# A two-layer decoder trunk in split float32: the order of the rounded-weight and remainder products within a weight piece

## The reference

```python
for i in range(DEPTH):                      # DEPTH = 2
    h = _rmsnorm(x, attn_norm_g[i])
    # layer 0: stick-breaking attention, layer 1: sparse attention with a top-k of keys
    x = x + mix
    h = _rmsnorm(x, ffn_norm_g[i])
    x = x + _conv_ffn(h, ffn_w_up[i], ffn_conv_w[i], ffn_conv_b[i], ffn_w_down[i])
```

## Time and profile before

| | before |
|---|---|
| median of three runs | 2218.34 us (2217.62 to 2219.71) |
| span of the profiled execution, first to last instruction | 2216.0 us |
| what lies between that span and the median | 2.3 us |
| PE busy | 2209.4 us, 12470 matmuls |
| PEld busy | 1935.2 us, 12470 loads |
| DVE busy | 1484.4 us |
| ACT busy | 1177.3 us |
| bytes read from memory | 408.42 MB, 185 GB/s over the span |
| granted TensorE clock | 1.000 of full speed over the span |

### The profile page before, as it was taken

How to read it: one execution, slowest core, us unless ns; L and a number is a source line. 1 busy time by engine, 2 the same in 40 slices (tenths; PEclk the granted TensorE clock), 3 DMA queues, 4 the chain that set the end, 5 groups by cost and what they waited for, 6 DMA issues and landing times.

```text
span 2216.0 us, 34772 instructions
## 1 busy us (share of the span) xinstructions
PE 2209.4 (100%) x12470; PEld 1935.2 (87%) x12470; DVE 1484.4 (67%) x1753; ACT 1177.3 (53%) x1409; POOL 14.3 (1%) x21
## 2 busy tenths in 40 slices
PE   9999999999999999999999999999999999999999
PEld 8888898888888888888899888888888888888887
DVE  7666556677777777555578888667777777774443
ACT  7565555555555555444455466555555555553333
POOL 0000000000000000000010000000000000000000
PEclk9999999999999999999999999999999999999999
DMA  7555555555555555565566544555555656566664
GB/s 270 166 168 177 171 162 181 195 185 190 189 193 186 189 190 191 190 190 189 191 212 198 177 157 139 161 183 191 182 198 181 194 184 198 180 193 201 201 199 136
DMA packets 113829, 411.55 MB, mean 186 GB/s; under 512 B 12769, under 2 KB 13537, under 8 KB 113761
## 3 DMA queue, kind: packets, MB, share of 16 engines
q1 hardware_dynamic: 112320, 406.70, 56.5%
q10 hardware_dynamic: 1008, 2.30, 0.3%
q0 software_dynamic: 432, 1.57, 0.2%
HBM read 408.42 MB, written 2.10 MB: 185 GB/s over the span
## 4 chain that ended last, share of the span: by engine, by line
PE 99%; DMA 0%; SPq 0%; DVE 0%; ACT 0%; issue 0%; DVEq 0%
PE psum L1301 99%; DMA raw<-w_all 0%; PE psum L1621 0%; PE psum L1557 0%; DVE w_lo L747 0%; ACT w_hi L289 0%; SPq L237 0%; SPq L235 0%; DVE upad L822 0%; SPq L236 0%; SPq L234 0%; DVEq L83 0%
## 5 line engine op out<-in xcount | busy, mean ns | idle before, releaser
L747 DVE TENSOR_TENSOR w_lo<-raw,w_hi 128x1024 fp32r<-128x1024 f32 x769 | 935.6, 1224 | 678.6 <-ACT w_hi L289 672.8
L1301 PE MATMUL psum<-xg,w_hi 128*128 128x512 f32 (+1 forms) x3936 | 1358.3, 392 | 1.9 <-DVE w_lo L747 1.0
L289 ACT CAST w_hi<-raw 128x1024 fp32r<-128x1024 f32 x770 | 803.1, 1049 | 771.4 <-PE psum L1301 767.6
L1301 PE MATMUL psum<-xg,w_lo 128*128 128x256 f32 (+1 forms) x3920 | 1090.8, 278 | 0.0
L1301 PEld LDWEIGHTS psum<-xg,w_hi 128*128 128x128 f32 x3936 | 736.0, 187 | 156.7 <-issue 2.2
L1301 PEld LDWEIGHTS psum<-xg,w_lo 128*128 128x128 f32 x3920 | 742.6, 189 | 2.6 <-issue 2.2
L1301 PE MATMUL psum<-hid,w_hi 128*128 128x512 f32 x704 | 244.1, 391 | 0.0
L1301 PE MATMUL psum<-w_hi,hid 128*128 128x512 f32 x704 | 217.9, 390 | 0.0
L1301 PE MATMUL psum<-hid,w_lo 128*128 128x256 f32 x704 | 197.4, 280 | 0.0
L1301 PE MATMUL psum<-att,w_hi 128*128 128x512 f32 x512 | 178.8, 393 | 0.0
L1301 PEld LDWEIGHTS psum<-hid,w_hi 128*128 128x128 f32 x704 | 131.7, 187 | 28.6
(11 more groups left out here) (176 smaller groups left out, 1062.9 us busy)
## 6 DMA issues: line engine op xcount, KB each, us to landing
raw<-w_all SPq DMA_DIRECT2D x770, 512.0 KB, 3.8
xres<-x_in SPq DMA_DIRECT2D x3, 512.0 KB, 9.0
cst<-consts_in ACTq DMA_DIRECT2D x2, 768.0 KB, 6.6
raw<-w_all SPq DMA_DIRECT2D x2, 256.0 KB, 3.6
xres<-x_in SPq DMA_DIRECT2D x2, 256.0 KB, 3.8
out_t<-part POOLq DMA_DIRECT2D x1, 512.0 KB, 7.3
out_t<-conv POOLq DMA_DIRECT2D x1, 512.0 KB, 7.4
out_t<-gates POOLq DMA_DIRECT2D x1, 512.0 KB, 7.0
```

What stands on the lines that cost most here:

```text
L289: act.copy(w_hi[:, c % RING, :], raw[:, c % RING, :]).then_inc(hi_ready, 1)
L747: dve.tensor_tensor(w_lo[:, c % RING, :], raw[:, c % RING, :], f32(w_hi[:, c % RING, :]), ALU.subtract).then_inc(lo_ready, 1)
L1301: return pe.matmul(o, lhsT, rhs, start=start, stop=True, skip_group_check=True)
```

## The change

Within `proj` the two products of a tile no longer follow each other. One loop over the eight tiles issues all products with `w_hi`, a second loop over the same tiles all products with `w_lo`. The waits for `xg_tile`, for `lo_ready` in the first piece and for `upper_free` stand in the first loop. `last`, which raises `piece_used`, is the last short product as before. No other function is touched.

```diff
                 s = c % RING
-                for ct in range(cols // P):
-                    if ct == 2 and upper_free is not None:
+                tiles = [(ct, kk) for ct in range(cols // P) for kk in range(kts)]
+                for ct, kk in tiles:
+                    if ct == 2 and kk == 0 and upper_free is not None:
                         pe.wait_ge(*upper_free)
-                    for kk in range(kts):
-                        w = slice(kk * cols + ct * P, kk * cols + (ct + 1) * P)
-                        k = k0_ + kk
-                        if by_tile and ct == 0 and kk == 2:
-                            pe.wait_ge(lo_ready, c + 1)
-                        if by_tile and ct == 0:
-                            pe.wait_ge(xg_tile, kk + 1)
-                        mm(psum[:, bank0 + ct, :], w_hi[:, s, w], act_in[:, k, :], first and kk == 0)
-                        last = mm(psum[:, bank0 + ct, 0:T], w_lo[:, s, w], act_in[:, k, 0:T])
+                    if by_tile and ct == 0 and kk == 2:
+                        pe.wait_ge(lo_ready, c + 1)
+                    if by_tile and ct == 0:
+                        pe.wait_ge(xg_tile, kk + 1)
+                    w = slice(kk * cols + ct * P, kk * cols + (ct + 1) * P)
+                    mm(psum[:, bank0 + ct, :], w_hi[:, s, w], act_in[:, k0_ + kk, :], first and kk == 0)
+                for ct, kk in tiles:
+                    w = slice(kk * cols + ct * P, kk * cols + (ct + 1) * P)
+                    last = mm(psum[:, bank0 + ct, 0:T], w_lo[:, s, w], act_in[:, k0_ + kk, 0:T])
                 last.then_inc(piece_used, 1)
```

## The result

The changed kernel takes 2227.96 us (median of five runs, 2227.63 to 2228.24) against 2217.62 us for the kernel before beside it: ratio 1.0046, 95% interval 1.0035 to 1.0057. It is slower by 10.3 us, where no difference that can be measured was forecast, and 3 us above the stated range.

The account below looks back on a forecast made before the run. TensorE's start-to-start gaps were taken to bound the kernel. Regrouping was worth 0 in steady stretches, edges and waits 0: 2216.0 us span less 2.3 is 2213.7, plus 2.3 to the median gives 2216.0 us, range 2208 to 2225.

Parts of the forecast that it names:

- pure gaps: Start-to-start gaps on TensorE among products of one length: 226.7 ns for 512 columns, 120.0 ns for 256; 2773 ns a piece.
- slow threes: About 115 stretches where three alternating pairs take 1.06 us, 20 ns lost each; forecast to go, gaining 2.3 us.
- The wait moved in layer 1's output projection: First piece, ahead of the fifth long product, now reached about 1385.89 us; cost forecast 0, at most 0.4 us.
- the edges of the runs: Where short and long runs meet in a piece: forecast between -7 and +10 ns a piece, taken as 0.
- Rival 2: Slower: the local pattern of 353.3 ns a pair takes hold at every edge from short to long; 2248.5 us, chance 0.10.
- the full pattern: 353.3 ns a pair instead of 346.67 taking hold everywhere: 6.67 ns x 4880 = 32.5 us.
- The reason given for 0: At a piece's edges, what a product gains at one edge it has lost at the other in the alternation also.
- The waits at the head: First piece: up to three short products (0.36 us) fall behind waits for the normed input's rows; cost forecast 0.
- the cover of 1.17 us: Time PE waits anyway behind the first piece for the next piece's remainders, set against 0.36 us of moved products.
- The rule on load shares: Busy share of weight loads measures TensorE's nearness to its limit; short runs would then have gaps of 188 ns.

## Why the prediction was wrong

**What held.** PE's gaps bind, waits played no part, and the pure gaps are what they were read as: 227 ns and 120 ns come back late in each run. The slow threes went, as forecast. The wait moved in layer 1's output projection cost nothing; no such wait is in the trace.

**The step that failed** is the edges of the runs: "Added, the two edges of a piece lie between -7 and +10 ns by the nearest rows [...] I take 0, because what a product gains at one edge it has lost at the other in the alternation also." Measured, they add to +20 ns. Each edge was read for one gap, and that gap was read rightly: the long run begins with 233 ns, some 6 over, and the short one with 113, 7 under. What failed is that the edge was taken to end there. In the changed kernel the long run needs five gaps to come down to 227 ns (28 ns lost), while the short run gets back 8. The sum was off too: 3 to 6 ns over and 3 to 10 under add to between -7 and +3 ns, and no row gives the +10.

The trace before had a place to read further, where long products of the value projection follow two short ones. Timeline of PE in the kernel before:

```profile
161.98 0.40 PE L1301 MATMUL psum<-w_hi,xg 128*128 128x512 f32 x1
...
162.91 0.39 PE L1301 MATMUL psum<-w_lo,xg 128*128 128x512 f32 x1
...
163.59 0.39 PE L1301 MATMUL psum<-w_lo,xg 128*128 128x512 f32 x1
```

The first four gaps take 0.93 us instead of 0.91, 29 ns more by the records; the next three are pure, 0.68 us. The same place at 87.98 us has 10 ns. Long edges of 10 to 29 ns, less the 3 to 10 read for the short edge, give 0 to 26 ns a piece, an estimate of 0 to 16 us.

Rival 2 named the place, "every edge from short to long", and its test, whether the second and third long products come over 230 ns apart; they come 236 apart. With its price at 20 ns, between the +10 of the edge and the 53 of the full pattern, it would have had the time: 2218.3 - 2.3 + 12.2 = 2228.2 us.

**The reason given for 0 failed as well.** It took the alternation as the sum of two pure gaps by nature. That sum, 346.67 ns, is one of two courses: without the throw-away products the same order runs at 353.3 ns for hundreds of microseconds. The trace before held the warning, since out of a pure short run the alternation fell into the slow course at once, and rival 2 cited 43.19 us for that.

**The waits at the head** were given 0 us; 0.3 were seen, in an execution whose input tile came 1.1 us later than before, so the cover of 1.17 us was used up. Runs don't settle whether that is the change's.

**The rule on load shares** (the Trainium skill, Perfetto Trace Analysis, section Identifying the Most-Contended Engine) would not have told the two orders apart: the share is 87% in the profile of either kernel, and short runs hold 120 ns.

**What stays open.** What the engine keeps from one product to the next is not known. The tolls at 256 columns come in steps of 6.7 ns (13, 20, 33 a piece; 20 per slow three), and neither edges, nor lengths of runs, nor slack for the loads give them all. What in the throw-away products sets the quick course, and whether one pair would do, wasn't tried. Leaving them out also moves all that follows 0.7 us earlier, and no run moves it without leaving them out.

No version beat the kernel before. With the quick course everywhere it would be 2.3 us lower, less than a measurement tells.

## What to carry to other kernels

Where TensorE is busy end to end, a product's gap can depend on the products before it. Here gaps read from pure runs did not add up in a mixed order, and an order's quick course hung on something far ahead of it. Before regrouping, read every gap of one transition until it has settled. The sum times the count of transitions is a first estimate only, since tolls of runs didn't simply add. Mixed lengths mostly paid, in either order; 512 columns throughout did not.

## What was not expected of the hardware

- The alternation of 512 and 256 columns has two lasting courses, 346.7 and 353.3 ns a pair; with or without six throw-away products (0.7 us) in each layer's first up-projection it runs in one or the other, at 410 us for all products up to 1142 us; the two groups are worth 21 us (2217.74 against 2238.86).
- The weight loads are recorded as 100% busy in a run of short products without a toll inside the run (120.0 ns a gap), and slack at 320 columns leaves the toll of an edge at 20 ns.
- A mixed order can lose up to 14 ns a pair (400 columns alternating: 3368 ns a piece, pure gaps 3253).
